# An encoder step on one Trainium2 core: layer-1 attention that scales its outputs instead of its probabilities, with the value products one unit behind the transposes, and modulation sums spread one to a tile

## What is computed

```python
def dsa_mixer(h, pos, w_in, w_out, past):          # layer 1
    q, k, v, qi, ki, wi = split_cols(h @ w_in, A_WIDTHS)
    ...
    def block(qp, qb, qib, wib):
        rel = relu(einsum('bqhd,bsd->bqhs', qib, ki_all))       # 8 index heads
        score = einsum('bqhs,bqh->bqs', rel, wib)
        _, idx = lax.top_k(score, topk)                         # selected keys
        logit = einsum('bqgrd,bqkgd->bqgrk', qg, k_sel) * HEAD_DIM ** -0.5
        p = softmax(logit, axis=-1)
        return einsum('bqgrk,bqkgd->bqgrd', p, v_sel)           # 16 heads of 64
    return sweep_queries(block, ...) @ w_out, ...

def run_trunk(x, c, ...):
    cs = silu(c)
    for i in range(DEPTH):
        sh1, sc1, gt1, sh2, sc2, gt2 = split(cs @ w_ada[i] + b_ada[i], 6)
        h = rms_norm(x) * (1 + sc1) + sh1
        x = x + gt1 * mixer(h)
        x = x + gt2 * swiglu(rms_norm(x) * (1 + sc2) + sh2)
    # one more shift and scale from w_ada_final before the output
```

## Time and profile before

| what | value |
|---|---|
| three timed runs | 1737.43, 1741.09, 1747.53 us; median 1741.09 |
| the profiled execution, its own time | 1747.03 us |
| its span, from first to last instruction | 1745.2 us |
| mean granted TensorE clock | 0.955 of full |
| busy: PE, PEld, DVE, ACT, POOL | 92%, 84%, 40%, 30%, 41% |

### The profile page before, as it was taken

How to read it: one execution, slowest core, us unless ns; L and a number is a source line. 1 busy time by engine, 2 the same in 40 slices (tenths; PEclk the granted TensorE clock), 3 DMA queues, 4 the chain that set the end, 5 groups by cost and what they waited for, 6 DMA issues and landing times.

```text
span 1745.2 us, 29777 instructions
## 1 busy us (share of the span) xinstructions
PE 1607.0 (92%) x11802; PEld 1469.2 (84%) x11802; DVE 698.2 (40%) x1432; ACT 525.0 (30%) x952; POOL 714.6 (41%) x360
## 2 busy tenths in 40 slices
PE   5888977798999699999988999998889999999997
PEld 3657833488999699999977888887789999999996
DVE  2548734413566565565154444444341111111113
ACT  1334244423222112222243343343232221122223
POOL 2214977643554234555522222224433343333451
PEclk9899979888999899999988999999989999999998
DMA  8544422013454555553224334332122223222221
GB/s 284 171 164 139 117 61 103 1 49 109 140 161 132 187 168 175 159 177 116 55 55 110 100 88 115 103 106 62 49 61 85 81 85 99 61 85 84 86 84 54
DMA packets 240948, 188.50 MB, mean 108 GB/s; under 512 B 12504, under 2 KB 228224, under 8 KB 233584
## 3 DMA queue, kind: packets, MB, share of 16 engines
q1 hardware_dynamic: 228720, 181.49, 34.4%
q10 hardware_dynamic: 12160, 6.09, 1.2%
HBM read 175.44 MB, written 8.50 MB: 105 GB/s over the span
## 4 chain that ended last, share of the span: by engine, by line
PE 78%; DVE 6%; issue 4%; ACT 4%; POOL 3%; DMA 3%; SPq 1%; ACTq 0%; DVEq 0%; POOLq 0%
PE lin L569 66%; PE O L811 2%; PE S L762 1%; ACT pr_a L1199 1%; PE T L791 1%; PE O L603 1%; POOL w_lo L1428 1%; DMA w_raw<-in_w_ffn_out 1%; DMA permb<-rawb 1%; DVE pr_a L1729 1%; PE T L848 1%; DVE acc L1857 1%; DVE pT_a L1779 1%; POOL qo L1475 1%; PE T L641 1%
## 5 line engine op out<-in xcount | busy, mean ns | idle before, releaser
L1428 POOL TENSOR_TENSOR w_lo<-w_raw,w_hi 128x1024 fp32r<-128x1024 f32 (+2 forms) x186 | 517.4, 2782 | 802.7 <-ACT w_hi L1053 802.7
L569 PE MATMUL lin<-act_hi,w_hi 128*128 128x288 f32 (+1 forms) x2464 | 372.7, 305 | 17.3 <-ACT act_hi L1083 12.1
L569 PEld LDWEIGHTS lin<-act_hi,w_hi 128*128 128x128 f32 (+1 forms) x2464 | 348.7, 194 | 28.5 <-issue 23.7
L569 PE MATMUL lin<-act_hi,w_lo 128*128 128x288 f32 (+1 forms) x2464 | 364.1, 298 | 0.9 <-POOL w_lo L1428 0.9
L569 PE MATMUL lin<-act_lo,w_hi 128*128 128x288 f32 (+1 forms) x2464 | 360.4, 297 | 0.0
L569 PEld LDWEIGHTS lin<-act_hi,w_lo 128*128 128x128 f32 (+1 forms) x2464 | 338.3, 188 | 8.5 <-issue 5.1
L569 PEld LDWEIGHTS lin<-act_lo,w_hi 128*128 128x128 f32 (+1 forms) x2464 | 339.7, 189 | 5.6 <-issue 4.8
L1053 ACT ACTIVATE w_hi<-w_raw 128x1024 fp32r<-128x1024 f32 (+2 forms) x186 | 204.6, 1100 | 189.7 <-PE lin L569 104.5
L1857 DVE SCALAR_TENSOR_TENSOR acc<-ada_raw,cs_w,acc 128x2048 f32<-128x2048 f32 x56 | 171.1, 3099 | 0.0
L1817 DVE SCALAR_TENSOR_TENSOR x<-lin,mods,x 128x288 f32 (+1 forms) x144 | 51.2, 412 | 290.1 <-PE lin L569 290.1
L1832 DVE TENSOR_TENSOR hf<-sg,lin 128x576 f32<-128x576 f32 x44 | 33.2, 754 | 313.5 <-PE lin L569 313.5
(11 more groups left out here) (244 smaller groups left out, 1378.6 us busy)
## 6 DMA issues: line engine op xcount, KB each, us to landing
ada_raw<-in_w_ada SPq DMA_DIRECT2D x44, 1024.0 KB, 5.4
w_raw<-in_w_ffn_in SPq DMA_DIRECT2D x88, 512.0 KB, 3.9
w_raw<-in_w_ffn_out SPq DMA_DIRECT2D x32, 704.0 KB, 4.6
w_raw<-in_w_in_b SPq DMA_DIRECT2D x32, 512.0 KB, 4.1
w_raw<-in_w_in_a SPq DMA_DIRECT2D x16, 512.0 KB, 4.5
ada_raw<-in_w_ada_final SPq DMA_DIRECT2D x8, 1024.0 KB, 7.0
bk<-cum_dram SPq DMA_DIRECT2D x16, 416.0 KB, 5.8
w_raw<-in_w_out_a SPq DMA_DIRECT2D x8, 512.0 KB, 3.6
```

The costliest lines, as they stand in the source:

```text
L569: last = nc.tensor.matmul(lin[0:m, u % 2, h, 0:HALF], w, (lo if p == 2 else hi)[:, t, tok], start=(p == 0 and t == 0), stop=(p == 2 and t ...
L1428: TT(w_lo[:, u % 2, 0:n], w_raw[:, u % 2, 0:n], w_hi[:, u % 2, 0:n].bitcast(F32), ALU.subtract)\
```

## The change

1. **Index stage.** `rel` has two buffers, so relu n waits for the scores of n - 2 and not n - 1. PE makes three modulation steps in each of the four units instead of two, and the transposes of block 1 stand inside the stage.
2. **Steps of block 2** (16 to 23): four are in the index stage, one each behind U_V, U_V+1, U_Q+1, U_Q+2. None is left in attention.
3. **Attention.** `norm_a` is gone from POOL. DVE takes the reciprocal of the two row sums spread over 64 columns each (`rbc`, 128 x 128), PE transposes it to a bank `R`, and DVE multiplies the whole pair's output by it once (`out_a`), behind ACT's copy. The transposes wait only for the exponential. The logits of n + 2 are made ahead of the transposes of n, and the values of n - 1 (`pva_unit`) behind them.
4. **Modulation sums.** The first six of DVE's 32 steps stand between the residual tiles of the mixer's output projection; steps 6 to 15 at FFN tiles 0 to 9 of half 0, 16 to 23 at its output units, 24 to 31 at tiles 0 to 7 of half 1. Collect 4 follows the first output unit, and collect 5 the last output unit of half 0.

```diff
 # SP
-            for n in range(KT + 2, KT + 4):
-                ada_load(n, ada_src(1, n - KT))
+            ada_next(10, 12)
             rope_swap(U_QI + 2)
+            ada_next(12, 13)
             w_load(U_V, wa[:, 1280:1280 + P], KT, P)
-            for n in range(KT + 4, KT + 6):
-                ada_load(n, ada_src(1, n - KT))
+            ada_next(13, 15)
             rope_swap(U_QI + 3)
+            ada_next(15, 16)
...
+            for m in range(KT):
                 w_load(U_OA + m, i["w_out_a"][0][:, m * P:(m + 1) * P], KT, P)
+                if m < 3:
+                    rope_swap(U_Q + PAIRS - 3 + m)
+                if m < OA_SLOTS:
+                    ada_sum_load(m)
 # PE, index stage
                     idx_unit(4 * j + c)
-                    if c % 2 == 0:
-                        ada_step(KT + 2 * j + c // 2)
+                    if c < 3:
+                        ada_step(KT + 3 * j + c)
+                    if (j, c) == (3, 0):
+                        ada_transpose(1, T_ADA1)
 # PE, attention
+            def pva_unit(n):
+                k, pair = n % 4, n // 4
+                pe.wait_ge(t_free, T_A + n + 1)
+                pe.wait_ge(t2_free, n + 1)
+                pe.wait_ge(rinv_done, n + 1)
+                if k == 0 and pair >= 1:
+                    pe.wait_ge(o_free, pair)
+                nc.tensor.transpose(R[:, k * P:(k + 1) * P], rbc[:, k, :], ident)
...
             for n in range(4 * PAIRS):
+                if n + 2 < 4 * PAIRS:
                     s_wait(n + 2)
+                    sa_unit(n + 2)
                 ta_unit(n)
-                if more:
-                    sa_unit(n + 2)
-                if n % 3 == 1 and n < 3 * KT:
-                    ada_step(2 * KT + n // 3, adaO)
-                pe.wait_ge(t2_free, n + 1)
...
+                if n >= 1:
+                    pva_unit(n - 1)
+            pva_unit(4 * PAIRS - 1)
+            pe.wait_ge(o_free, PAIRS)
 # PE, FFN of layer 1
             ffn_half(U_F0, ACT_N1, 0, None, lambda: ada_collect(3), after_first)
-            ada_collect(4)
+            ada_collect(5)
 # ACT
                 if n >= 1:
-                    act.wait_ge(sc_step, 2 * n)
-                A(rel[0:rows, :, 0:nk], S[0:rows, :, 0:nk], ACT.Relu).then_inc(rel_done, 1)
+                    act.wait_ge(sc_step, 2 * n - 2)
+                A(rel[0:rows, n % 2, :, 0:nk], S[0:rows, :, 0:nk], ACT.Relu).then_inc(rel_done, 1)
 # POOL
-            for n in range(4 * PAIRS):
-                norm_a(n)
...
+            rope(U_Q + PAIRS - 1)
+            for pair in range(PAIRS - 1):
+                split_pair(pair)
 # DVE, attention
-                V.reciprocal(rinv[:, k, 0:w], rowsum[:, k, 0:w]).then_inc(rinv_done, 1)
+                if k == 0:
+                    V.reciprocal(rinv[:, 0, 2:3], rowsum[:, 0, 2:3])
+                V.reciprocal(rbc[:, k, :].rearrange("p (e c) -> p e c", e=2),
+                             rowsum[:, k, 0:2].rearrange("p (e a) -> p e a", a=1).broadcast_to([P, 2, 64]))\
+                    .then_inc(rinv_done, 1)
+            def out_a(n):
...
+                if k == 3:
+                    dve.wait_ge(o_copied, 2 * pair + 2)
+                    V.tensor_tensor(qo[:, pair, 0:NP_], qo[:, pair, 0:NP_], R, ALU.mult).then_inc(o_free, 1)
...
             for n in range(4 * PAIRS):
+                recip_a(n)
+                if n + 2 < 4 * PAIRS:
+                    max_unit((n + 2) % 4, n + 2, ...)
+                if n >= 1:
+                    out_a(n - 1)
                 ta_evac(n)
-                if n + 2 < 4 * PAIRS:
-                    max_unit((k + 2) % 4, n + 2, ...)
 # DVE, modulation sums
-            residual(U_OA, 16)
+            for m in range(KT):
+                residual_tile(U_OA, 16, m)
+                if m < OA_SLOTS:
+                    ada_sums(m)
```

240 lines of the change are left out of this document (124 added, 116 removed).

## The result

The changed kernel took 1712.97 us (median of 4 runs, 1710.71 to 1718.19), the kernel before 1741.55 us beside it. The ratio is 0.9838, with a 95% interval from 0.9801 to 0.9874. The forecast was 1713.4 us.

What follows compares the result with a forecast made beforehand. Bounds named: PE in FFN tiles, a ring of waits in layer-1 attention, PE idle at index stage and first FFN output units. Terms sum to -27.7 us from 1747.0: 1719.3, or 1713.4 on the median; range 1696 to 1733.

Steps and rivals of the forecast that it cites:

- Index stage, +7.0: Index stage: second relu buffer -7.3, four modulation steps +4.2, transposes +0.5, three waits for loads behind row swaps +9.6 us.
- -7.3 for the second relu buffer: Index stage: PE's waits of 3.55, 1.47 and 2.24 us for relu would go with two buffers.
- Up to attention, +3.3 and -6.9: V and Q units: four added steps less 0.87 us hidden, +3.3; first transposes no longer wait for POOL, -6.9 us.
- Attention, -29.0: Layer-1 attention: 13.5 us a pair, plus 1.5 for first turns, makes 109.5 instead of 138.5 us.
- that is the floor: Layer-1 attention: DVE's 11.6 us of work a pair, as the fullest engine, was taken as the least a pair needs.
- Rival D: Layer-1 attention: PE and DVE take turns, about 20 us a pair, total +24, 1765 us; chance 0.07.
- Output projection, +8.2: Output projection: DVE's sums and POOL's splits exclude each other, 8.2 us a tile, residual 7 at about 53 instead of 44.8.
- FFN half 0, -20.3: First FFN output units: one step a tile removes the gaps, so 45.7 of 66.0 us remain.
- Collect 5, +8.5: Behind half 0's last output unit: PE waits 5.8 us uncovered for step 23, plus 2.7 for the clock.

Runs made afterwards that it cites:

- e1: Changed kernel with three index-stage modulation loads issued ahead of the row swaps; 1702.41 us, ratio 0.979 to the kernel before.
- e7: Changed kernel with one relu buffer in the index stage instead of two; 1711.39 us, ratio 0.9827 to the kernel before.
- e4: Changed kernel with DVE's layer-1 attention reciprocal writing two columns instead of 128; span 1702.4 us against 1710.2, 12.23 us a pair against 12.74.
- e10: Changed kernel with output scaling by DVE kept, but all engines in the order of the kernel before in attention; 1740.02 us, ratio 1.0001.
- e11: Changed kernel with the new attention order kept, but POOL scaling the probabilities again; 1748.44 us, ratio 1.0036 to the kernel before.
- e6: Changed kernel with each attention unit's values in the same turn, right behind its own transposes; 1765.21 us, ratio 1.0127 to the kernel before.
- e2: Changed kernel with collect 5 moved behind the first two units of FFN half 1; 1705.68 us, ratio 0.9802 to the kernel before.
- e3: Changed kernel with the 32 modulation sums and the collects where the kernel before had them; 1714.76 us, ratio 0.9869.
- e8: Changed kernel with two sums in the output projection, one at every tile of both FFN halves, collects as before; 1701.74 us, ratio 0.9781.
- e9: Changed kernel with five output-projection modulation steps made plain one-input products; first projection matmul to first FFN matmul 63.4 us against 68.7.

## Why the prediction was right, and where it was not

**Index stage, +7.0 against +10.9.** The mechanism was right: three waits for a load behind the row swap, 2.55, 2.51 and 3.40 us, 8.5 in all against 9.6; e1 shows that it is the swap. What the term lacked is the first unit, 2.77 us, whose load I had taken for hidden. I took the median of 5.7 us from issue to landing for all of them, and this one took 8.7; before, the wait for relu had covered it. Another 0.78 us came at the last load, and 1.6 us are the clock: the matmuls behind the waits ran at the half clock for a while, which cost about 3.0 us in the kernel before and about 4.6 in the changed one (their rows against the same rows at the full clock). And e7 shows that one half of the term was mis-booked: -7.3 for the second relu buffer is not a gain of its own but shares its time with the loads' waits.

**Up to attention, +3.3 and -6.9 against +1.8 and -3.9.** The four steps were there, but they covered more of PE's waits than the 0.87 us that I counted: two waits for ACT's copies of keys shrank by 0.5 us each (the first of them from 2.57 to 2.10 us). The wait for POOL went, as forecast, but not to nothing: 1.82 us were left for the exponential of the sample's logits, and the logits of unit 2, which now stand ahead of the first transposes, took 1.2 us with a short wait ahead of them.

**Attention, -29.0 against -33.1.** 12.74 us a pair against my 13.5, and a granted clock of 1.00 in the steady part; the first turns and the last pair, part of it at the half clock, took 3.5 us on top of eight such pairs, where I had 1.5. The value was near, the reason given for it was not: "that is the floor", said of DVE's 11.6 us, does not stand against e4. DVE has 11.1 us a pair (66.39 / 76 x 12.74) and PE 11.4, and the 1.3 us on top are hand-overs. The prediction's own figures had it: some 10 us for PE at the full clock and five transposes, of 0.27 us each as it turned out, make as much as DVE's work. What I had not priced at all is that the gain needs both halves (e10, e11): the sum spoke of POOL's link alone, as if its removal carried the gain. Rival D, PE and DVE taking turns, had a price of 20 us a pair and 1765 us in all; e6, which puts the values back behind their own transposes, gives 20.3 us and 1765.21. The mechanism is D's, since the two do take turns there, but that the numbers meet is in part luck: PE's own part was 15.1 us a pair at a clock of 0.79 (70.53 / 95 x 20.3), and the reciprocals, which D had in the turn, ran beside it. It is the unit of delay that excludes the rival.

**Output projection, +8.2 against +4.7.** Up to the sums of squares it was 62.67 against 55.61 us, +7.1; from the second wait on the tiles were 8.0 and 8.2 us apart (368.95, 376.93 and 385.09 us), as worked out. The norm's small matmuls behind it then gave 2.4 back: 6.07 us instead of 8.43, at a granted clock of 0.77 instead of 0.53. The same matmuls ran at the half clock in e2, from the third row on in e3 and from the fifth in e7, and at the full one in e1 and e8; what decides it was not settled. So the projection itself cost 7.1 us of the 8.2 forecast, and the norm's clock, which no term had, took 2.4 back. e9 shows that the term is the sums on DVE: with a one-input product in their place 1.4 of the 7.1 us are left. Whether it is the second input that costs it, e9 doesn't settle, since it also makes the instruction shorter. By the Trainium skill (SBUF — State Buffer, Who interferes with whom) a DVE instruction with two SBUF inputs and a GpSimd one that reads SBUF shut each other out. The rows of the changed kernel agree: sums of 3.46 us instead of 2.34, squares of 2.76 instead of 1.43. The rows of e9 add that products with one input are held up as well, and hold POOL up. The same section allows it, as it names `tensor_scalar` among the forms that can take the shared pair in a two-port mode. That a product takes 1.28 us where a sum takes 2.34 fits such a mode, but no row names it.

**FFN half 0, -20.3 against -21.2.** Right: no gap, and e3, with the sums where they were, brings three gaps back.

**Collect 5, +8.5 against +7.5.** The wait was 5.68 us against 5.8; the half clock then held for the collect itself (1.72 us) and few matmuls more, not for 22. e2 takes the whole term away.

**What follows.** 3.1 us that no term had. The small matmuls of two later norms took 1.7 and 1.0 us less, at a higher clock, and the rest is spread; no run was made for it.

Over all, the median met the forecast by 0.4 us, but the sum of terms did not meet the profile as closely: -35.0 against -27.7 us. The index stage and the first wait cost 6.9 us more than forecast, the six other terms 11.1 us less, and 3.1 us were not booked. That the median hides this 7.3 us is chance. The terms were made against a profiled execution that lay 5.5 us above the median of its kernel, and that of the changed kernel lies 0.8 us under its own; these 6.3 us are most of the 7.3. Of the four parts of the change, attention carries the gain. The move of the sums gives at most some us as it stands (e3 against the changed kernel: 1714.76 and 1712.97), and 11 us more if four steps stay out of the projection; the place of the new loads behind the swaps costs 10 us.

## What to carry to other kernels

When a ring runs over four engines, taking one link out (POOL's product) or taking the copies off PE's path (values one unit behind) can each be worth next to nothing, and both together 4.3 us of a pair's 17.1: try them as a pair before dropping either, and price what the ring would be with each alone. A load that is moved in a queue of transfers must be read with what stands ahead of it there, here a swap that waits for a unit's end; put it ahead of the waiting transfer. And spread work over the tiles of a stage that has room by moving only the steps that are too many: two here, not six into a stage where two engines get in each other's way.

## What the runs showed of the chip that was not expected

- A wait on PE can cost more than its length, but does not always: the eight modulation matmuls behind waits of 2.55 and 2.51 us took 1.66 and 1.94 us instead of 1.06, those behind 3.40 us took 1.06, and the sixteen of collect 5, behind 5.68 us, took 3.64 us instead of 1.92 (changed kernel).
- POOL's square next to DVE's sums with two inputs took 2.76 us, with one input 1.94, alone 1.43; DVE's two-input sum took 3.46 us there, 3.18 on the mean of the FFN and 2.34 at its shortest, and the one-input product 2.19 there and 1.28 at its shortest.
- With PE waiting at each unit (e6) the granted clock was 0.79 over 95 us of attention; in the steady part of the changed kernel it was 1.00.
